# First convolution taps and two key scalings from VectorE to ScalarE, with both queues re-ordered, in a two-layer hybrid decoder step

## The chip, the cores and the metric

One core of one Trainium2 chip. The metric is the device time of one launch in microseconds (us); the median of the runs shown is what changes are judged by.

## The reference

A step of a decoder trunk of two layers over 320 tokens: a prompt of 256 and 8 sequences of 8 tokens with states. A layer is

```python
x = x + 0.5 * _swiglu(_rmsnorm(x, norm_ffn1), ...)
proj = _rmsnorm(x, norm_mix) @ w_in                  # split into four groups
o = concat[_rwkv7_group, _rglru_group, _gdn_group, _gla_group]
x = x + o @ w_out
x = x + 0.5 * _swiglu(_rmsnorm(x, norm_ffn2), ...)
```

The change touches two of the groups. In `_rwkv7_group`:

```python
kk = _l2norm(_heads(k * lp['rwkv_k_k'], HEAD_DIM))
k = k * (1.0 + (a - 1.0) * lp['rwkv_k_a'])
```

and in `_gdn_group` the causal convolution with `CONV_K = 4` taps over the 768 columns of q, k and v, ahead of a silu. All is float32.

## The kernel before

**Tiling.** Activations stand with their features on the 128 partitions and the 320 tokens along the free axis. Weights come in units of 128x1024 (eight blocks of 128x128), 166 units a layer: 66 for the first feed-forward part, 26 for the input projection (tiles 0 to 25 in this text), 8 for the output projection, 66 for the second feed-forward part. A float32 product is made of three matmuls on operands that are split in a high part (`wh`, `xh`) and a low part (`wl`, `xl`), lines L479 to L481; a tile of 128 output columns has 8 x 3 = 24 matmuls over 320 columns.

**How a unit gets there.** SyncE loads it to `raw` (a ring of four, from tile 14 on in two of these places) when the low part of the unit before in that place has been made. ScalarE copies it to `wh` (`split_hi`, L1186) when TensorE has used the unit that stood there four units earlier. VectorE subtracts to get `wl` (`split_lo`, L1592). TensorE waits for `lo_ready`, the count of low parts made. In the mixing stage `ahead(m)` makes the split of tile m + 4, on ScalarE and on VectorE alike: `ahead(5)` is the split of tile 9.

**The mixing stage** begins with the input projection. TensorE's order is written out by hand: tiles, with the small products of the four groups between them. Of its first part:

```python
tile_mm(layer, IN0 + 8, 0)
half_tile(layer, 9, 0)
rw_products(layer)
half_tile(layer, 9, 1)
...
rw_rows(layer)
...
tile_mm(layer, IN0 + 11, 1)
inverse_t(layer, 0, 1)
```

`half_tile(9, 0)` waits for the evacuation of tile 7 (`in_read` 8) and for the split of tile 9. Tiles 4 and up take turns in two banks, so tile m waits for the evacuation of tile m - 2. VectorE and ScalarE have orders written out by hand too, each a queue in which nothing is passed. VectorE's steps in the opening are: `evac(m)` (out of PSUM with the norm's factor, L1663 and L1664; it waits for tile m), `rw_mix` (token shift, L1683 to L1688), `rw_keys_raw` (L1693), `rw_keys` (L1696 to L1702), `rw_decay` (L1712, L1714), `rw_scaled` (L1718 to L1724), `gla_floor` (L1833, which waits for ScalarE's `gla_ab`, L1408), `rw_rest` (L1728, L1729; its products are read by `rw_products`), `rw_masks` (L1740, behind `rw_products`), `gdn_gate` (L1764 to L1770), `inverse(0, l)` (L1975, L1982 and a transpose L1967), `rw_reads` (L1707), `gdn_conv(j)` (the first tap L1752, the other three L1749), `gla_decay` (L1837, L1839). ScalarE's are: sigmoids (L1385, L1388), `kk_sq` (L1391), exponentials and logarithms of the decay and the key norm (L1393 to L1404, the last of them signals `kk_rn`), `gla_ab` behind `ahead(7)`, `eye(0)` (L1276, which waits on the count of splits up to tile 13, because it writes to places of the raw ring), the moves of `rw_rows` (L1292 and six times L1287), `inverse_t` (L1258) and `across` (L1266, L1267; `across(0, 1)` waits for `gla_decay`).

Of the kernel before, what the change touches and what calls it, by code (L numbers as in the profile page):

```python
# [16 lines left out]
ACT = mybir.ActivationFunctionType  # L17
ALU = mybir.AluOpType
# [5 lines left out]
NC = TOK // CH  # L24
# [4 lines left out]
CONV = 4  # L29
# [19 lines left out]
T_RW, T_SMALL, T_GDN, T_GLA, T_RG, T_Z, T_GT, T_RGG = 0, 3, 8, 14, 18, 20, 22, 24  # L49
# [30 lines left out]
def columns(spec):  # L80
# [28 lines left out]

MIX_SIGNALS = {  # L110
    "padded": ("pads", "rg_pads"), "xm": 7, "lora_in": 1, "lora_mm": 3, "sg": 2, "ra": 2,
    "rw_gc": 2, "shift_kept": 1, "kkraw": 2, "kk_sq": 1, "rkr": 2, "head_sums": ("kk_sum", "rk_sum", "gdn_sum"), "cum": 2, "prev": 1,
    "rw_P": 1, "kk_rn": 1, "rb": 1, "rw_ops": 1, "kPi": 1, "bPi": 1, "bonus": 1,
    "rw_pairs": 2, "rw_pairs_read": 6,
    "rw_rows_mm": 3, "rw_rows": 3, "conv": 6, "gdn_act": ("beta", "sp_dt", "cqk", "gsq", "cq", "gdn_ln", "gdn_rn"),
    "gates": 1, "gcum": 1, "gdn_spread": ("Gb_mm", "Gc_mm", "bb_mm"), "Gb": 2, "eG": 1,
# [8 lines left out]
    "hcen": 1, "yo": 1, "ysq0": 1, "ysq1": 1, "ysq2": 1, "cent_mm": 1, "cent_read": 1, "yrs": 3, "var_mm": 3, "VM": 4, "dec_mm": 3,  # L125
    "dec_decay": 3, "var_read": 3, "dec_add": 5, "sq_sum": 3,
}
V_STEPS, A_STEPS, G_STEPS = 102, 51, 14 + 3 * 6
G_ALL = DEPTH * G_STEPS - 6


# [44 lines left out]
def program(nc, xT, wts, par, cst, sin, mst, yT, sout, mout):  # L176
    with ExitStack() as ctx:
# [38 lines left out]
        def P(name, i=0, n=1):  # L216
            return pr[:, PAR[name][0] + i:PAR[name][0] + i + n]
# [90 lines left out]
        def chunked(v):  # L308
            return v.rearrange("q p (c t) -> q c p t", c=NC)
# [72 lines left out]
        S = {}  # L382
# [18 lines left out]
        def on(eng, layer, s, k=None):  # L401

            s = S[s] if isinstance(s, str) else s
            apart(eng, s, s.upto(layer, k)) if eng.engine in OWN_WAITS else eng.wait_ge(s.sem, s.upto(layer, k))
# [775 lines left out]
        def _(act):  # L1180
# [59 lines left out]
            for layer in range(DEPTH):  # L1240
                st = Steps(act, a_step, layer, plain)

                def say(ins, name):
                    return st(ins, S[name])
# [4 lines left out]
                def ahead(*ms):  # L1249
                    for m in ms:  # L1250
                        split_hi(layer, IN0 + RING + m)

                def inverse_t(g, l):
                    on(act, layer, f"inv_mm{g}", 2 * l - 1)
                    dst, src = pairs_of(Tm[g], l), products_of(l)
                    if l > 1:
                        dst, src = halves(dst, 1 << l, 0), halves(src, 1 << l, 0)
                    say(act.activation(dst, src, ACT.Copy), f"T{g}")  # L1258

                def across(g, l):  # L1260

                    on(act, layer, f"XY{g}", 2 * l - 1)
                    if (g, l) == (0, 1):
                        on(act, layer, "ltm_read")
                    n = chunks_of(l)
                    st(act.activation(Yx[g][half[1], 0:n], Y[g][half[0], NC:NC + n], ACT.Copy))  # L1266
                    say(act.activation(Yx[g][half[0], 0:n], Y[g][half[1], NC:NC + n], ACT.Copy), f"across{g}")  # L1267
# [5 lines left out]
                def eye(g):  # L1273
                    if g == 0:
                        act.wait_ge(lo_ready.sem, layer * UNITS + IN0 + LATE)
                    say(act.activation(Y[g], lev[:, 0, :].unsqueeze(1).broadcast_to([128, 10, CH]), ACT.Copy), f"eye{g}")  # L1276
# [5 lines left out]
                def home(dst, bank, name=None):  # L1282

                    for p in range(2):
                        for to, at in pieces(p):
                            d, n = dst[to, :, p, :], dst.shape[1]
                            ins = act.activation(d, ps[at, bank + p, 0:n * CH].rearrange("q (c t) -> q c t", c=n), ACT.Copy)  # L1287
                            say(ins, name) if name and to is half[1] else st(ins)
# [6 lines left out]
                def log_sums(dst, n):  # L1295
# [4 lines left out]
                            say(ins, "gdn_ln") if n == 4 and k == 1 and to is half[1] else st(ins)  # L1300
                    st.settle()

                def decode_out(g):
                    on(act, layer, "R0_mm", g + 1)
                    home(dec_out[g], 6, "R0T")
# [81 lines left out]
                for p in range(2):  # L1387
                    say(act.activation(ra[:, p, :], ps[:, 6 + p, 0:TOK], ACT.Sigmoid, bias=P("a0", p)), "ra")  # L1388
                ahead(4)
                act.wait_ge(S["kkraw"].sem, S["kkraw"].upto(layer))  # L1390
                say(act.activation(rsq[:], kk[:], ACT.Square), "kk_sq")  # L1391
                act.preload_act_table_set("natural_log_exp_and_others")
                st(act.activation(tiny[R, 10:11], P("alog")[R], ACT.Exp))  # L1393
                st(act.activation(lnt[R, :], small[R, :], ACT.Abs, bias=P("dtb")[R]))
                st(act.activation(tiny[:, 11:13], P("lam", 0, 2), ACT.Abs))
                ahead(5)
                act.wait_ge(S["cum"].sem, S["cum"].upto(layer))
                st(act.activation(rP[:], cum[:], ACT.Exp, scale=-WDEC))
                st(act.activation(Pinv[:], cum[:], ACT.Exp, scale=WDEC))
                act.wait_ge(S["prev"].sem, S["prev"].upto(layer))  # L1400
                say(act.activation(Pprev[:], sg[:], ACT.Exp, scale=-WDEC), "rw_P")
                act.wait_ge(S["kk_sum"].sem, S["kk_sum"].upto(layer))
                log_sums(rsq, 2)
                say(act.activation(rsq[:], rsq[:], ACT.Exp, scale=-0.5), "kk_rn")  # L1404
                ahead(6)
                ahead(7)
                on(act, layer, "gla_z")
# [10 lines left out]
                say(act.activation(tiny[:, 11:13], tiny[:, 11:13], ACT.Ln, bias=C("one")), "sp_lam")  # L1418
                say(act.activation(ltm, ltm, ACT.Ln, bias=C("one")), "gla_ln")
                ahead(8)  # L1420
                ahead(9)
                ahead(10)
                eye(0)
                on(act, layer, "rw_rows_mm", 1)
                rows_of(rVt, 2, "rw_rows")
                on(act, layer, "rw_rows_mm", 2)
                home(kLt, 4, "rw_rows")
                on(act, layer, "rw_rows_mm", 3)
                home(bLt, 6, "rw_rows")
                act.wait_ge(S["Gb_mm"].sem, S["Gb_mm"].upto(layer))  # L1430
                for p in range(2):
                    say(act.activation(Gb[:, p, :], ps[:, 6 + p, 0:TOK], ACT.Copy), "Gb")
                ahead(11)
                inverse_t(0, 1)
                across(0, 1)
                on(act, layer, "Gb")
                say(act.activation(eG[:], Gb[:], ACT.Exp), "eG")
                ahead(12)
                ahead(13)
                across(0, 2)  # L1440
                inverse_t(0, 2)
                act.wait_ge(S["conv"].sem, S["conv"].upto(layer, 4))
# [142 lines left out]
        def _(ve):  # L1585
# [62 lines left out]
            for layer in range(DEPTH):  # L1648
                st = Steps(ve, v_step, layer, plain)

                def say(ins, name):
                    return st(ins, S[name])
# [22 lines left out]
                def ahead(*ms):  # L1675
                    for m in ms:
                        split_lo(layer, IN0 + RING + m)
# [10 lines left out]
                        say(stt(seqs(xm[:, k, :], 0), seqs(xm[:, k, :], 0), P("mu", k), seqs(rwp[:, k, :], 1, 1), ALU.mult, ALU.add), "xm")  # L1688
                    st.settle()

                def rw_keys_raw():
                    for p in range(2):
                        say(ts(kk[:, p, :], xm[:, 2 + p, :], P("kk", p), -1.0, ALU.mult, ALU.mult), "kkraw")  # L1693

                def rw_keys():
                    st(ts(tiny[:, 13:15], P("ka", 0, 2), -1.0, 1.0, ALU.mult, ALU.add))  # L1696
                    on(ve, layer, "ra")
                    st.settle()
                    for p in range(2):
                        st(ts(kmod[:, p, :], ra[:, p, :], P("ka", p), tiny[:, 13 + p:14 + p], ALU.mult, ALU.add))  # L1700
                    st.settle()
                    st(tt(kmod[:], kmod[:], xm[:, 2:4, :], ALU.mult))  # L1702

                def rw_reads():
# [10 lines left out]

                def rw_scaled():
                    on(ve, layer, "kk_rn")
                    st(tt(kk[:], kk[:], rsq[:], ALU.mult))  # L1718
                    st.settle()
                    say(tt(ra[:], kk[:], ra[:], ALU.mult), "rb")  # L1720
                    on(ve, layer, "rw_P")
                    st(tt(kkr[:, :, :, 0, :], chunked(kk), chunked(Pprev), ALU.mult))
                    on(ve, layer, "rb")
                    say(stt(bPi[:], ra[:], -1.0, Pinv[:], ALU.mult, ALU.mult), "bPi")  # L1724

                def rw_rest():
                    on(ve, layer, "rw_P")
                    say(tt(kkr[:, :, :, 1, :], chunked(xm[:, 0:2, :]), chunked(rP), ALU.mult), "rw_ops")  # L1728
                    say(tt(kPi[:], kmod[:], Pinv[:], ALU.mult), "kPi")  # L1729
# [23 lines left out]

                def gdn_conv(j):
                    on(ve, layer, "shift_kept")
                    for k in range(CONV):
                        st.settle()
                        ins = tap(cv, gcp, j, 6, k, "gcw")
                        say(ins, "conv") if k == CONV - 1 else st(ins)

# [327 lines left out]
                evac(3)  # L2088
                rw_mix(2, 4)
                ahead(1)  # L2090
                rw_keys_raw()
                ahead(2)
                ahead(3)
                rw_decay()
                evac(4)
                rw_keys()
                evac(5)
                ahead(4)
                rw_mix(0, 2)
                ahead(5)  # L2100
                evac(6)
                rw_scaled()
                gla_floor()
                evac(7)
                rw_rest()
                ahead(6)
                evac(8)
                ahead(7)
                rw_mix(4, 6)
                ahead(8)  # L2110
                rw_masks()
                gdn_gate()
                ahead(9)
                evac(9)
                evac(10)
                ahead(10)
                inverse(0, 0)
                rw_reads()
                gdn_conv(0)
                gdn_conv(1)  # L2120
                gla_decay()
                evac(11)
                rw_gain()
                ahead(11)
# [411 lines left out]
```

## Time and profile before

| what | value |
|---|---|
| median of 3 runs | 1352.57 us (1351.97 to 1353.64) |
| profiled execution, its own time | 1353.87 us |
| its span | 1352.1 us, mean granted clock of TensorE 0.997 |
| busy: TensorE, VectorE, ScalarE, GpSimd | 1329.3, 855.8, 692.6, 77.4 us |
| weights read by SyncE's queue | 332 units of 512 KB |

The opening of the mixing stage, from the first evacuation to the end of the first group's inverse, lies at 255 to 330 us in layer 0 and at 922 to 997 in layer 1. Times of the trace count from the span's start. A timeline row has the start, the duration, engine, line and operation, and in brackets how long the engine had stood idle and what released it. Durations of neighbours overlap a little, so that what an instruction costs in a row of them is the distance between two starts. The end of a matmul is modelled.

### The profile page before, as it was taken

The numbers are of one execution on the slowest core, as the hardware profiler recorded it, in microseconds if no ns is written. First come the engines' busy times: TensorE is split into PE (matmuls) and PEld (weight loads), VectorE is DVE, ScalarE is ACT, GpSimd is POOL, SyncE is SP. The second block draws the span as 40 slices with busy tenths as digits, with TensorE's granted clock in tenths as the row PEclk, the third lists the DMA queues.
The fourth block names the chain that finished last, engine by engine and source line by source line (L and its number), as shares of the span: only waits on it lengthen the run. The fifth ranks groups of instructions, "written<-read, shape, count | busy, mean of one in ns | idle before, by whom it ended". The sixth has DMA issues, their size and how long they took to land.

```text
span 1352.1 us, 31424 instructions
## 1 busy us (share of the span) xinstructions
PE 1329.3 (98%) x12584; PEld 1289.2 (95%) x12584; DVE 855.8 (63%) x1327; ACT 692.6 (51%) x995; POOL 77.4 (6%) x113
## 2 busy tenths in 40 slices
PE   7999999999999999999999999999999999999997
PEld 7999999998988999999999999999888899999997
DVE  6656533898876756553376565349988766555533
ACT  7444423757655644443364444347466655454423
POOL 0000000200030100000010000001001310000001
PEclk9999999999999999999999999999999999999999
DMA  8544454322313644444454444443223244444541
GB/s 302 173 143 150 144 155 155 111 79 80 112 50 111 212 145 150 146 154 154 142 189 153 155 143 152 151 144 110 80 79 97 66 158 156 155 148 147 155 142 53
DMA packets 50768, 185.90 MB, mean 137 GB/s; under 512 B 5760, under 2 KB 6272, under 8 KB 50176
## 3 DMA queue, kind: packets, MB, share of 16 engines
q1 hardware_dynamic: 49104, 177.37, 41.3%
q10 hardware_dynamic: 1584, 7.35, 1.5%
q8 instruction: 63, 1.03, 0.3%
q14 instruction: 17, 0.14, 0.0%
HBM read 180.14 MB, written 4.56 MB: 137 GB/s over the span
## 4 chain that ended last, share of the span: by engine, by line
PE 86%; DVE 11%; issue 2%; ACT 1%; DMA 0%; DVEq 0%; ACTq 0%
PE ps L479 27%; PE ps L481 26%; PE ps L480 26%; DVE wl L1592 2%; DVE ar L1749 2%; PE ps L847 1%; DVE ar L1663 1%; PE ps L749 1%; PE ps L1035 0%; DVE raw L1967 0%; PE ps L817 0%; PE ps L1013 0%; PE ps L799 0%; DVE ar L1740 0%; DVE ar L1683 0%
## 5 line engine op out<-in xcount | busy, mean ns | idle before, releaser
L479 PE MATMUL ps<-xh,wh 128*128 128x320 f32 x1952 | 611.8, 313 | 9.0 <-DVE xl L1614 8.0
L1592 DVE TENSOR_TENSOR wl<-raw,wh 128x1024 fp32r<-128x1024 f32 x332 | 408.1, 1231 | 317.5 <-ACT wh L1186 317.1
L481 PE MATMUL ps<-xh,wl 128*128 128x320 f32 x1952 | 604.4, 310 | 0.0
L480 PE MATMUL ps<-xl,wh 128*128 128x320 f32 x1952 | 604.3, 310 | 0.0
L1186 ACT ACTIVATE wh<-raw 128x1024 fp32r<-128x1024 f32 x332 | 349.3, 1054 | 356.2 <-PE ps L481 339.1
L479 PEld LDWEIGHTS ps<-xh,wh 128*128 128x128 f32 x1952 | 367.5, 188 | 20.1 <-issue 9.0
L480 PEld LDWEIGHTS ps<-xl,wh 128*128 128x128 f32 x1952 | 367.7, 188 | 0.5
L481 PEld LDWEIGHTS ps<-xh,wl 128*128 128x128 f32 x1952 | 367.6, 188 | 0.0
L479 PE MATMUL ps<-hid_h,wh 128*128 (+1 forms) x704 | 217.5, 309 | 0.0
L480 PE MATMUL ps<-hid_l,wh 128*128 (+1 forms) x704 | 217.5, 309 | 0.0
L481 PE MATMUL ps<-hid_h,wl 128*128 (+1 forms) x704 | 217.5, 309 | 0.0
L1228 ACT ACTIVATE gus<-gus 128x320 f32<-128x320 f32 x88 | 41.6, 472 | 190.0 <-DVE gus L1631 190.0
L479 PEld LDWEIGHTS ps<-hid_h,wh 128*128 128x128 f32 x704 | 132.1, 188 | 0.0
L480 PEld LDWEIGHTS ps<-hid_l,wh 128*128 128x128 f32 x704 | 132.1, 188 | 0.0
L481 PEld LDWEIGHTS ps<-hid_h,wl 128*128 128x128 f32 x704 | 132.1, 188 | 0.0
L1631 DVE TENSOR_TENSOR gus<-ps,rstd 128x320 f32<-128x320 f32 x88 | 43.2, 491 | 97.0 <-PE ps L481 90.9
L2270 POOL TENSOR_TENSOR ar<-ar 128x320 f32<-128x320 f32 x35 | 30.7, 878 | 765.7 <-ACT ar L1211 758.0
L1228 ACT ACT_TABLE_LOAD x44 | 56.5, 1283 | 2.4 <-issue 1.6
L1635 DVE TENSOR_TENSOR gus<-gus 128x320 f32<-128x320 f32 x88 | 43.3, 492 | 16.0 <-ACT gus L1228 4.1
L1639 DVE TENSOR_TENSOR hid_l<-gus,hid_h 128x320 f32 x88 | 42.6, 484 | 0.0
L1632 DVE TENSOR_TENSOR gus<-ps,rstd 128x320 f32<-128x320 f32 x88 | 42.3, 481 | 0.0
L1614 DVE SCALAR_TENSOR_TENSOR xl<-x,pr,xh 128x320 fp32r<-128x320 f32 x48 | 39.5, 859 | 1.4 <-ACT xh L1210 1.4
(290 smaller groups left out, 934.6 us busy)
## 6 DMA issues: line engine op xcount, KB each, us to landing
raw<-wts SPq DMA_DIRECT2D x332, 512.0 KB, 3.5
ms<-mst ACTq DMA_DIRECT2D x2, 1440.0 KB, 7.9
mout<-ms ACTq DMA_DIRECT2D x2, 1440.0 KB, 6.6
x<-xT SPq DMA_DIRECT2D x4, 320.0 KB, 4.9
yT<-x SPq DMA_DIRECT2D x4, 320.0 KB, 2.4
cs<-cst SPq DMA_DIRECT2D x1, 652.0 KB, 8.1
pr<-par ACTq DMA_DIRECT2D x1, 429.0 KB, 4.2
pr<-par ACTq DMA_DIRECT2D x1, 425.0 KB, 5.3
```

The source lines that it names most:

```text
L479: pe.matmul(out, a, rh, start=start, stop=False)
L480: pe.matmul(out, a, rl, start=False, stop=False)
L481: return pe.matmul(out, b, rh, start=False, stop=stop)
L1186: act.activation(wh[:, s, :], raw_of(layer, n), ACT.Copy).then_inc(hi_ready.sem, 1)
L1228: act.activation(gus[:, m, :], gus[:, m, :], ACT.Silu).then_inc(sil_ready.sem, 1)
L1592: tt(wl[:, s, :], raw_of(layer, n), wh[:, s, :].bitcast(F32), ALU.subtract).then_inc(lo_ready.sem, 1)
L1614: stt(xl[:, k, :], x[:, k, :], P(name, k), xh[:, k, :].bitcast(F32), ALU.mult, ALU.subtract).then_inc(xl_ready.sem, 1)
L1631: tt(gus[:, m, :], ps[:, 2 * m, 0:TOK], rstd[:], ALU.mult).then_inc(gs_ready.sem, 1)
L1632: tt(gus[:, 2 + m, :], ps[:, 2 * m + 1, 0:TOK], rstd[:], ALU.mult).then_inc(gu_read.sem, 1)
L1635: tt(gus[:, m, :], gus[:, m, :], gus[:, 2 + m, :], ALU.mult).then_inc(act_ready.sem, 1)
L1639: tt(hid_l[:, at, :].rearrange("q a t -> q (a t)"), gus[:, m, :], hid_h[:, at, :].rearrange("q a t -> q (a t)").bitcast(F32), ALU.subtract ...
L2270: ins = gp.tensor_tensor(nsq[:, 0, :], nsq[:, 0, :], nsq[:, k, :], ALU.add)
```

## The change

- `kk_sq` is made on ScalarE from `xm` with the scale P("kk") in the square, in two instructions; VectorE's `rw_keys_raw` goes. `rw_scaled` multiplies the key in, in two instructions instead of one, and the sign moves from the key to `kkr` (two instructions instead of one) and out of `bPi`.
- The affine part of the modified key (`ka_mix`, two instructions of Identity with scale and bias) moves to ScalarE; VectorE keeps the small `rw_keys_rest` and one product.
- The first tap of each of the six convolution tiles (`first_tap(j)`, a Copy with a scale over 344 columns) moves to ScalarE. It waits for the evacuation of its tile and for a buffer. `gdn_conv(j)` waits for it and does taps 1 to 3.
- Both queues get another order. TensorE's, SyncE's and GpSimd's are as before.

```diff
@@ ScalarE
+                def first_tap(j):
+                    act.wait_ge(in_read.sem, in_read.upto(layer, T_GDN + j + 1))
+                    on(act, layer, "pads" if j < 3 else "bPi" if j < 5 else "rk_sum")
+                    say(act.activation(cv[:, j, 0:CVP - 3], gcp[:, j, 0:CVP - 3], ACT.Copy, scale=P("gcw", j)), "tap0")
...
-                act.wait_ge(S["kkraw"].sem, S["kkraw"].upto(layer))
-                say(act.activation(rsq[:], kk[:], ACT.Square), "kk_sq")
+                act.wait_ge(S["xm"].sem, S["xm"].upto(layer, 3))
+                for p in range(2):
+                    say(act.activation(rsq[:, p, :], xm[:, 2 + p, :], ACT.Square, scale=P("kk", p)), "kk_sq")
...
-                ahead(5)
                 act.wait_ge(S["cum"].sem, S["cum"].upto(layer))
                 st(act.activation(rP[:], cum[:], ACT.Exp, scale=-WDEC))
                 st(act.activation(Pinv[:], cum[:], ACT.Exp, scale=WDEC))
+                on(act, layer, "ra")
+                on(act, layer, "ka_rest")
+                for p in range(2):
+                    say(act.activation(kmod[:, p, :], ra[:, p, :], ACT.Identity, scale=P("ka", p), bias=tiny[:, 13 + p:14 + p]), "ka_mix")
...
                 say(act.activation(rsq[:], rsq[:], ACT.Exp, scale=-0.5), "kk_rn")
+                ahead(5)
                 ahead(6)
                 ahead(7)
...
                 ahead(8)
+                first_tap(0)
                 ahead(9)
+                eye(0)
                 ahead(10)
-                eye(0)
                 on(act, layer, "rw_rows_mm", 1)
                 rows_of(rVt, 2, "rw_rows")
...
                 home(bLt, 6, "rw_rows")
+                first_tap(1)
+                inverse_t(0, 1)
+                across(0, 1)
+                first_tap(2)
...
                 ahead(11)
-                inverse_t(0, 1)
-                across(0, 1)
...
                 ahead(12)
+                first_tap(3)
+                first_tap(4)
                 ahead(13)
+                first_tap(5)
@@ VectorE
-                def rw_keys_raw():
-                    for p in range(2):
-                        say(ts(kk[:, p, :], xm[:, 2 + p, :], P("kk", p), -1.0, ALU.mult, ALU.mult), "kkraw")
+                def rw_keys_rest():
+                    say(ts(tiny[:, 13:15], P("ka", 0, 2), -1.0, 1.0, ALU.mult, ALU.add), "ka_rest")
...
                 def rw_keys():
...
-                    for p in range(2):
-                        st(ts(kmod[:, p, :], ra[:, p, :], P("ka", p), tiny[:, 13 + p:14 + p], ALU.mult, ALU.add))
-                    st.settle()
+                    on(ve, layer, "ka_mix")
                     st(tt(kmod[:], kmod[:], xm[:, 2:4, :], ALU.mult))
...
                     on(ve, layer, "kk_rn")
-                    st(tt(kk[:], kk[:], rsq[:], ALU.mult))
+                    for p in range(2):
+                        st(stt(kk[:, p, :], xm[:, 2 + p, :], P("kk", p), rsq[:, p, :], ALU.mult, ALU.mult))
...
-                    st(tt(kkr[:, :, :, 0, :], chunked(kk), chunked(Pprev), ALU.mult))
+                    for p in range(2):
+                        st(stt(kkr[:, :, p, 0, :], kk[:, p, :].rearrange("q (c t) -> q c t", c=NC), -1.0,
+                               Pprev[:, p, :].rearrange("q (c t) -> q c t", c=NC), ALU.mult, ALU.mult))
...
                 rw_mix(2, 4)
                 ahead(1)
-                rw_keys_raw()
+                rw_keys_rest()
                 ahead(2)
                 ahead(3)
                 rw_decay()
                 evac(4)
-                rw_keys()
                 evac(5)
                 ahead(4)
                 rw_mix(0, 2)
-                ahead(5)
                 evac(6)
+                rw_keys()
                 rw_scaled()
                 gla_floor()
                 evac(7)
                 rw_rest()
+                ahead(5)
+                evac(8)
                 ahead(6)
-                evac(8)
+                rw_mix(4, 6)
                 ahead(7)
-                rw_mix(4, 6)
-                ahead(8)
                 rw_masks()
                 gdn_gate()
+                ahead(8)
+                evac(9)
                 ahead(9)
-                evac(9)
                 evac(10)
+                inverse(0, 0)
                 ahead(10)
-                inverse(0, 0)
+                gla_decay()
                 rw_reads()
                 gdn_conv(0)
                 gdn_conv(1)
-                gla_decay()
                 evac(11)
```

## Rows read from the trace of the kernel before

**Rows 1.** The page's first part: busy time, share of the span, instructions.

```profile
PE 1329.3 (98%) x12584; PEld 1289.2 (95%) x12584; DVE 855.8 (63%) x1327; ACT 692.6 (51%) x995; POOL 77.4 (6%) x113
```

**Rows 2.** TensorE's waits over the span: total us, times, longest us.

```profile
PE ps L904 <- issue: 1.2, 1, 1.2
PE ps L799 <- DVE raw L1967: 1.0, 2, 0.5
...
PE ps L479 <- DVE ar L1664: 1.0, 2, 0.5
...
PE ps L817 <- ACT ar L1267: 0.7, 2, 0.4
```

**Rows 3.** Busy time by stretch: PE, PEld, DVE, ACT, POOL, clock, DMA.

```profile
255.00:330.00 75.00, 73.61 (x880) 66.10 (x879) 71.63 (x140) 49.44 (x80) 3.66 (x9) 1.00 0.29 93
330.00:382.00 52.00, 52.00 (x1176) 46.75 (x1176) 43.17 (x87) 31.78 (x61) 7.71 (x13) 1.00 0.30 94
```

**Rows 4.** TensorE's timeline, 278 to 329 us.

```profile
278.71 0.31 PE L479 MATMUL ps<-xh,wh 128*128 128x320 f32 x1
...
293.02 0.41 PE L479 MATMUL ps<-xh,wh 128*128 128x320 f32 x1 [0.49 <-DVE ar L1664]
...
296.74 0.81 PE L799 MATMUL ps<-raw,ar 64*64 64x64 f32 x40
...
303.61 0.27 PE L817 MATMUL ps<-raw 64*64 64x64 f32 x2 [0.37 <-ACT ar L1267]
...
328.01 0.69 PE L799 MATMUL ps<-raw,ar 64*64 64x64 f32 x32 [0.53 <-DVE raw L1967]
```

**Rows 5.** Groups by line and form: busy us, mean ns of one.

```profile
L1210 ACT ACTIVATE xh<-x,pr 128x320 fp32r<-128x320 f32 x8 | 4.5, 558 | 1.0 <-DVE x L1595 1.0
...
L1752 DVE TENSOR_SCALAR ar<-ar,pr 128x344 f32<-128x344 f32 x6 | 2.4, 399 | 0.5
```

**Rows 6.** ScalarE's timeline, 275 to 277 us.

```profile
275.45 1.06 ACT L1186 ACTIVATE wh<-raw 128x1024 fp32r<-128x1024 f32 x1 [2.11 <-PE ps L481]
276.42 0.51 ACT L1408 ACTIVATE ar<-ps,pr 128x320 f32<-128x320 f32 x1
```

**Rows 7.** VectorE's timeline, 277 to 280 us.

```profile
277.35 0.54 DVE L1833 TENSOR_SCALAR ar<-ps,pr 128x320 f32<-128x320 f32 x1
277.81 0.41 DVE L1663 TENSOR_TENSOR ar<-ps,rstd 128x256 f32<-128x256 f32 x1
...
278.27 0.81 DVE L1728 TENSOR_TENSOR ar<-ar 128x640 f32<-128x640 f32 x1
...
279.74 1.31 DVE L1592 TENSOR_TENSOR wl<-raw,wh 128x1024 fp32r<-128x1024 f32 x1
```

**Rows 8.** VectorE's timeline, 282 to 292 us.

```profile
282.56 0.68 DVE L1683 TENSOR_TENSOR ar<-ar 128x512 f32<-128x512 f32 x1
...
284.79 1.22 DVE L1592 TENSOR_TENSOR wl<-raw,wh 128x1024 fp32r<-128x1024 f32 x1
285.93 3.13 DVE L1740 TENSOR_TENSOR ar<-ps,cs 128x512 f32<-128x512 f32 x6
289.10 0.38 DVE L1764 TENSOR_SCALAR ar<-ar,pr 4x320 f32<-4x320 f32 x1
...
291.28 1.22 DVE L1592 TENSOR_TENSOR wl<-raw,wh 128x1024 fp32r<-128x1024 f32 x1
```

**Rows 9.** ScalarE's timeline, 292 to 297 us.

```profile
292.54 0.74 ACT L1276 ACTIVATE raw<-cs 128x640 f32<-128x640 f32 x1 [0.76 <-DVE wl L1592]
293.18 0.69 ACT L1292 ACTIVATE ar<-ps 128x640 f32<-128x640 f32 x1
293.76 2.72 ACT L1287 ACTIVATE ar<-ps 128x320 f32<-128x320 f32 x6
```

**Rows 10.** Busy time by stretch in layer 1; the clock is the third number from the end.

```profile
995.00:1000.00 5.00, 4.97 (x48) 4.30 (x49) 3.04 (x4) 4.85 (x8) 0.00 (x0) 0.71 0.61 204
1000.00:1005.00 5.00, 5.00 (x61) 4.74 (x60) 2.51 (x6) 3.34 (x5) 0.00 (x0) 0.95 0.01 2
```

More of the change, by code:

```diff
@@ L111 @@
     "padded": ("pads", "rg_pads"), "xm": 7, "lora_in": 1, "lora_mm": 3, "sg": 2, "ra": 2,
-    "rw_gc": 2, "shift_kept": 1, "kkraw": 2, "kk_sq": 1, "rkr": 2, "head_sums": ("kk_sum", "rk_sum", "gdn_sum"), "cum": 2, "prev": 1,
-    "rw_P": 1, "kk_rn": 1, "rb": 1, "rw_ops": 1, "kPi": 1, "bPi": 1, "bonus": 1,
+    "rw_gc": 2, "shift_kept": 1, "kk_sq": 2, "rkr": 2, "head_sums": ("kk_sum", "rk_sum", "gdn_sum"), "cum": 2, "prev": 1,
+    "rw_P": 1, "kk_rn": 1, "rw_keyed": ("rb", "bPi", "rw_ops", "kPi"), "ka_mix": 2, "ka_rest": 1, "tap0": 6, "bonus": 1,
     "rw_pairs": 2, "rw_pairs_read": 6,
@@ L127 @@
 }
-V_STEPS, A_STEPS, G_STEPS = 102, 51, 14 + 3 * 6
+V_STEPS, A_STEPS, G_STEPS = 95, 51, 14 + 3 * 6
 G_ALL = DEPTH * G_STEPS - 6
@@ L1689, in rw_mix @@
                     st.settle()
-                def rw_keys_raw():
-                    for p in range(2):
-                        say(ts(kk[:, p, :], xm[:, 2 + p, :], P("kk", p), -1.0, ALU.mult, ALU.mult), "kkraw")
+                def rw_keys_rest():
+                    say(ts(tiny[:, 13:15], P("ka", 0, 2), -1.0, 1.0, ALU.mult, ALU.add), "ka_rest")
                 def rw_keys():
-                    st(ts(tiny[:, 13:15], P("ka", 0, 2), -1.0, 1.0, ALU.mult, ALU.add))
-                    on(ve, layer, "ra")
-                    st.settle()
-                    for p in range(2):
-                        st(ts(kmod[:, p, :], ra[:, p, :], P("ka", p), tiny[:, 13 + p:14 + p], ALU.mult, ALU.add))
-                    st.settle()
+                    on(ve, layer, "ka_mix")
                     st(tt(kmod[:], kmod[:], xm[:, 2:4, :], ALU.mult))
@@ L1721, in rw_scaled @@
                     on(ve, layer, "rw_P")
-                    st(tt(kkr[:, :, :, 0, :], chunked(kk), chunked(Pprev), ALU.mult))
+                    for p in range(2):
+                        st(stt(kkr[:, :, p, 0, :], kk[:, p, :].rearrange("q (c t) -> q c t", c=NC), -1.0,
+                               Pprev[:, p, :].rearrange("q (c t) -> q c t", c=NC), ALU.mult, ALU.mult))
                     on(ve, layer, "rb")
-                    say(stt(bPi[:], ra[:], -1.0, Pinv[:], ALU.mult, ALU.mult), "bPi")
+                    say(tt(bPi[:], ra[:], Pinv[:], ALU.mult), "bPi")
                 def rw_rest():
@@ L1755, in gdn_conv @@
                     on(ve, layer, "shift_kept")
-                    for k in range(CONV):
-                        st.settle()
+                    on(ve, layer, "tap0", j + 1)
+                    for k in range(1, CONV):
+                        if k > 1:
+                            st.settle()
                         ins = tap(cv, gcp, j, 6, k, "gcw")
```

## The prediction

> **What bounds the kernel now.** I read the page first. TensorE is busy 98% of the span [rows 1], so a change can give back only what TensorE loses, and can cost only what it makes TensorE lose. The second view is the list of TensorE's waits [rows 2]: three of them lie in the opening of the mixing stage, where this change is, each once per layer. The third is the busy time by stretch [rows 3]: in the 75 us of the opening (255 to 330) TensorE lacks 75.00 - 73.61 = 1.39 us and VectorE is busy 71.63 of 75, ScalarE 49.44. In the next 52 us VectorE has nearly 9 us free. So in the opening TensorE and VectorE run side by side with almost no play. The timeline shows where TensorE is held, in brackets behind a row [rows 4]: 0.49 us ahead of tile 11 (for `evac(9)`), 0.37 us ahead of `inverse_y(0, 1)` (for `across(0, 1)`, which waits for `gla_decay`), 0.53 us ahead of `inverse_t(0, 4)`. Sum 1.39 us a layer, 2.8 us in all: that is the most that the opening can give, 0.2% of the time, as long as the clock is the same.
>
> **What the change takes off VectorE.** A start-to-start distance is what an instruction costs in a row of them. Two key scalings (an estimate of 0.7 us at nearly the price of a first tap; a small instruction takes their place), two affine instructions (0.8), six first taps at 0.40 us and a short settling each (2.6) [rows 5]: 3.9 us less with the small one taken off. `rw_scaled` gets two instructions for one at two places, some 0.2 us more each. Net VectorE is 3.4 us shorter a layer. That alone would more than pay the 1.39 us.
>
> **What it puts on ScalarE.** An instruction over 320 columns with its scale read from a tile took 0.558 us [rows 5]; so six taps 3.4 us, `ka_mix` 1.1, and `kk_sq` 0.3 more. The trace has no Identity with scale and bias both from a tile: bounds 0.46 and 0.65, I take 0.56. ScalarE has 25 us free in the opening, so the 4.8 us are hidden, unless one stands ahead of something due. `kk_rn` does not come later: `ahead(5)`, 0.95 us, now stands behind it and pays for `ka_mix`.
>
> By the Trainium skill, "ScalarE: Activation LUTs", Rules for kernel authors, a multiplication belongs on VectorE and not on ScalarE. The rows agree as to the price, 0.40 us against 0.56. By that rule alone the six taps lose 1 us a layer; by the sum here they cost nothing where ScalarE is idle.
>
> **The new order: a wait at tile 9.** TensorE starts half tile 9 only when its split is done, and `ahead(5)` is that split. Before, VectorE made it ahead of `evac(6)` and TensorE ran through from tile 8, with the first matmul of tile 9 at 278.71 [rows 4]. Now `ahead(5)` stands behind `rw_keys`, `rw_scaled`, `gla_floor`, `evac(7)` and `rw_rest`, while TensorE's order is the same. When does VectorE come to it?
> - `evac(6)` waits for tile 6. Tile 7 ended at 275.4 (it released ScalarE's split [rows 6]) and a tile takes 3.5 us (tile 11 has 296.74 - 293.02 = 3.72 with 0.1 of switching at either end [rows 4]), so tile 6 ends at 271.9. From there `evac(6)` 0.46, `rw_keys` 0.74, the two key instructions 1.0, `rb` 0.74, two for `kkr` 1.0, `bPi` 0.74: 276.6. 0.46 is the distance of one evacuation and 0.74 that of a 640-column instruction, half of `rw_rest`'s 1.47 [rows 7]; the 1.0 are estimates at 0.5 for an instruction of 320 columns, between 0.40 and 0.58. The strided pair for `kkr` isn't in the trace; between 0.48 and 0.8 each, I take 0.5; the low end changes nothing here and the high end adds 0.3 us of wait.
> - `gla_floor` needs `gla_ab` of ScalarE, which ends at 276.42 + 0.51 = 276.93 and hangs on tile 7 by way of `ahead(7)` [rows 6], unchanged. So VectorE, arriving at 276.6, waits until 276.94.
> - `gla_floor` and `evac(7)` 0.92, `rw_rest` 1.47, the split 1.2 to 1.3 [rows 7]: 276.94 + 0.92 + 1.47 + 1.23 = 280.56.
>
> TensorE goes on at 280.6 and not at 278.71: **1.9 us lost**, and 0.1 for the restart (the first matmul behind a wait takes 0.41 instead of 0.31 us [rows 4]). It is 2.0 us behind. Even if `gla_ab` were early, VectorE's own work would leave 1.6 us.
>
> **A second wait, at `inverse_t(0, 1)`.** It needs ScalarE's `rw_rows`, which now stand behind `eye(0)` and `ahead(10)`, and `eye(0)` waits for VectorE's `ahead(9)`. VectorE from 279.33 (the start of `ahead(5)`): split 1.14 (285.93 - 284.79), `evac(8)` 0.46, split 1.14, `rw_mix(4, 6)` 2.23, split 1.14, masks 3.17 and about 0.3 of wait for the second group of pair products (TensorE being late), `gdn_gate` 2.18, split 1.14, `evac(9)` 0.46, split 1.22 to its end [rows 7, 8]: 14.6 us, so 293.9. Then ScalarE: `eye(0)` 0.64 to the next start, the split 0.95, the rows 3.30 (293.18 to 293.76 + 2.72) [rows 9]: 298.8. They were done at 296.48. TensorE itself would be there at 296.74 + 2.0 - 0.49 = 298.25, because tile 11 no longer waits. So it waits 0.6 us and is then 2.1 us behind.
>
> **What comes back.** `gla_decay` is now ahead of the taps, so `across(0, 1)` is done at 301.5, while TensorE needs it at 305: the 0.37 us go. VectorE is back on the old times at 322 (its relief has been spent in waits for TensorE), and TensorE comes to `inverse_t(0, 4)` late: the 0.53 us go too. The load of raw tile 17 hangs on `ahead(11)`, which ends some 0.6 us later than before; its tile is due well after. First taps 3 to 5 wait for evacuations that come before ScalarE's next split is allowed by TensorE, so they hold up nothing. Behind 330 VectorE and ScalarE are the ones that wait, and the later waits in [rows 2] are chains through TensorE itself; nothing there takes up the rest. Balance per layer 2.0 - 0.49 + 0.6 - 0.37 - 0.53 = **1.2 us, 2.4 us in two layers**.
>
> **The clock.** After the wait at `inverse_t(0, 4)` of layer 1 and four thin matmuls, the granted clock fell to its lower level: 0.71 in one stretch of 5 us and 0.95 in the next [rows 10]. By the clock that is 5.00 x (0.29 + 0.05) = 1.7 us of full-clock work. The same place in layer 0 had no fall, so it is a matter of chance. The profiled execution took 1353.87 us, 1.30 over the median of 1352.57, so I take the median run as one without a fall. A wait of 1.9 us is over three times that of 0.53, and 0.6 us now stand just ahead of the thin matmuls of `gdn_decay`. I count one more fall in the median run at 1.6 us, with none to three as bounds.
>
> The Trainium skill, "TensorE: Matmul & The Clock Gate", The HAM clock gate, says that the array's clock is throttled by default and that activity releases it, with two levels only. The trace agrees with two levels; that rule would make the fall likelier with longer idling, as assumed above.
>
> **The forecast and the rivals.** A difference below 0.2%, 2.7 us, can't be told from none.
> - **A, 0.48: the wait at tile 9, and the clock falls more often.** 1352.57 + 2.4 + 1.6 = 1356.6, own range 1355.3 to 1359.6 (up to three falls).
> - **B, 0.27: the wait at tile 9, no more falls.** 1355.0. For it: a 1.2 us wait late in the recurrences [rows 2] had no fall behind it. Within 0.2%.
> - **C, 0.12: the relief reaches TensorE.** It decides at the start of `ahead(5)`: if VectorE gets there at 277.5 and not 279.3, nothing is lost at tile 9, and with it the second wait goes. The gain is then 1.39 us a layer, and layer 1's fall with its wait: 1352.6 - 2.8 = 1349.8 or less, faster. For it: VectorE's waits for TensorE could be shorter than I put them. Against it: `gla_ab` alone forbids 277.5.
> - **D, 0.13: ScalarE's queue becomes the path.** Its taps stand ahead of splits and of `rw_rows`; a tap that waits for an evacuation holds all behind it. Were `eye(0)`, `ahead(10)` and the rows another 1 us later, this adds 1 us a layer to A or B: 1357 to 1359. Slower. The table of rules named above points that way.
>
> **Slower** is A and D, 0.61; **the same** is B, 0.27; **faster** is C, 0.12. The range 1352.0 to 1359.6 leaves out most of C and the far end of D, and takes in a bound of one layer's balance near zero.
>
> **What would show it.** In the profile after, in both layers: a wait of TensorE for the split L1592 of about 1.9 us between the 72 matmuls of tiles 6 to 8 and the half tile, a wait for `rw_rows` ahead of L799 of about 0.6 us, and none of the three old ones. VectorE idle ahead of `evac(6)` for about 1 us and ahead of `gla_floor`. The prediction is wrong if half tile 9 starts without a wait, if VectorE runs ahead of these times, or if something behind 330 takes up the delay.

## The result and the profile after

The changed kernel took 1361.8 us (1357.09 to 1365.68, 7 runs) against 1352.77 (1351.97 to 1354.28, 7 runs) of the kernel before beside it: ratio 1.0063, 95% interval 1.0042 to 1.0083. It is slower by 9.0 us. The forecast was slower, but with 1356.6 us and no more than 1359.6: the sign holds and the size does not.

The profiled execution is the fastest of the seven, 1357.09 us, span 1355.2 us, mean clock 0.998.

The page's first part, which answers to [rows 1]:

```profile
PE 1329.4 (98%) x12584; PEld 1289.3 (95%) x12584; DVE 849.1 (63%) x1311; ACT 701.7 (52%) x1013; POOL 77.2 (6%) x113
```

TensorE is busy for the same time. What was added in this execution is idle time: 1355.2 - 1329.4 = 25.8 us against 22.8. VectorE has 6.7 us less to do, ScalarE 9.1 more. TensorE's waits, as in [rows 2]:

```profile
PE ps L479 <- DVE wl L1608: 3.9, 2, 1.9
PE ps L799 <- ACT ar L1287: 2.8, 2, 2.1
...
PE ps L904 <- issue: 0.6, 1, 0.6
```

The three waits of the old opening are gone, two new ones stand in their place, and both are the ones of the prediction. TensorE's timeline at them, layer 0 and then layer 1:

```profile
280.96 0.38 PE L479 MATMUL ps<-xh,wh 128*128 128x320 f32 x1 [1.93 <-DVE wl L1608]
...
299.24 0.81 PE L799 MATMUL ps<-raw,ar 64*64 64x64 f32 x40 [0.68 <-ACT ar L1287]
...
947.94 0.39 PE L479 MATMUL ps<-xh,wh 128*128 128x320 f32 x1 [1.94 <-DVE wl L1608]
...
967.66 0.81 PE L799 MATMUL ps<-raw,ar 64*64 64x64 f32 x40 [2.12 <-ACT ar L1287]
```

1.93 and 1.94 us were forecast as 1.9, and 0.68 as 0.6. But in layer 1 the second wait is 2.12 us. The chain of the work that ended last, followed through layer 1 up to that wait (start, duration, what), names what is new:

```profile
958.34 1.24 DVE wl L1608
959.58 0.02 issue
959.59 3.65 DMA raw<-wts
963.24 0.02 issue
963.26 1.06 ACT wh L1186
964.32 0.59 ACT ar L1292
```

`ahead(8)` on VectorE, the split of tile 12, ends at 959.58. Only then does SyncE load tile 14, which lands 3.65 us later; ScalarE has done `eye(0)` and stands before `ahead(10)`, which is tile 14's split, and behind it are the rows of `rw_rows` for which TensorE waits. ScalarE's timeline shows the stop, layer 0 without it and layer 1 with it:

```profile
294.21 0.74 ACT L1276 ACTIVATE raw<-cs 128x640 f32<-128x640 f32 x1 [3.63 <-DVE wl L1608]
294.85 1.04 ACT L1186 ACTIVATE wh<-raw 128x1024 fp32r<-128x1024 f32 x1
295.80 0.69 ACT L1292 ACTIVATE ar<-ps 128x640 f32<-128x640 f32 x1
296.39 2.71 ACT L1287 ACTIVATE ar<-ps 128x320 f32<-128x320 f32 x6
...
961.20 0.74 ACT L1276 ACTIVATE raw<-cs 128x640 f32<-128x640 f32 x1 [3.64 <-DVE wl L1608]
963.26 1.06 ACT L1186 ACTIVATE wh<-raw 128x1024 fp32r<-128x1024 f32 x1 [1.33 <-DMA raw<-wts]
```

Why only layer 1: up to tile 13 a unit goes to the raw place of its number modulo four, and tile 14 goes to place 0 in both layers. 66 units stand ahead of tile 0 in layer 0, 232 in layer 1, so the unit that last held place 0 is tile 10 in layer 0 and tile 12 in layer 1. Tile 12's split is one of those that the change moved, behind `gdn_gate`.

Busy time by stretch, for [rows 3] and beyond, first the kernel after, with its stretches in layer 1:

```profile
255.00:330.00 75.00, 72.39 (x877) 65.46 (x875) 68.32 (x133) 54.31 (x89) 3.76 (x9) 1.00 0.28 93
375.00:425.00 50.00, 47.90 (x1095) 41.34 (x1092) 35.85 (x81) 30.64 (x53) 13.21 (x17) 1.00 0.16 54
...
922.00:997.00 75.00, 70.95 (x829) 63.98 (x829) 66.48 (x131) 51.57 (x85) 3.73 (x9) 0.98 0.27 86
...
965.00:970.00 5.00, 2.88 (x53) 1.86 (x54) 4.79 (x9) 4.40 (x10) 0.00 (x0) 1.00 0.28 109
970.00:975.00 5.00, 5.00 (x29) 4.39 (x22) 3.65 (x7) 3.02 (x6) 0.00 (x0) 0.66 0.14 15
```

and then two more stretches of the kernel before (375 to 425 holds the recurrences of layer 0):

```profile
375.00:425.00 50.00, 47.07 (x1051) 40.72 (x1052) 35.96 (x80) 29.91 (x50) 13.21 (x17) 1.00 0.14 45
...
922.00:997.00 75.00, 73.61 (x881) 66.10 (x879) 71.67 (x140) 49.44 (x80) 3.68 (x9) 1.00 0.30 93
```

Layer 0's opening loses 73.61 - 72.39 = 1.22 us more than before, where the prediction had 1.2. Layer 1's opening loses 73.61 - 70.95 = 2.66 us more. Behind its long wait the clock fell: 0.66 over 5 us, which is 5.00 x 0.34 = 1.7 us of full-clock work. The kernel before had its one fall between 995 and 1005 [rows 10], so the openings of the two profiled executions have a fall each, and nearly all of the 1357.09 - 1353.87 = 3.2 us between them is idle time.

In the recurrences of layer 0 TensorE idles 2.10 us instead of 2.93, 0.8 us less. That is no effect of the delay as far as the traces show. `late12_alone` (below), whose opening of layer 0 is that of before, idles 1.71 us there (the first row), and a second execution of the changed kernel, `after_again`, 2.40 (the second):

```profile
375.00:425.00 50.00, 48.29 (x1096) 41.89 (x1091) 36.45 (x81) 31.29 (x52) 13.21 (x17) 1.00 0.14 45
375.00:425.00 50.00, 47.60 (x1089) 40.45 (x1086) 35.40 (x81) 29.96 (x52) 13.23 (x17) 1.00 0.16 53
```

The other runs of the changed kernel differ in the clock. A thousandth of the mean granted clock over 1,360 us is 1.4 us of full-clock work:

```
us      1357.09  1357.62  1361.03  1361.80  1363.30  1363.75  1365.68
clock   0.998    0.998    0.995    0.995    0.993    0.993    0.993
```

The median run has 0.003 less than the profiled one, 4.1 us by the clock (to within 1.4 us, as both are rounded to a thousandth), and is 4.7 us longer. So 9.0 us are: 3.2 of idle time in the profile, 4.7 from there to the median run of after, and 1.1 from the profiled run of before (which has a fall) down to its median.

### The profile page after: what moved, and what is told of

Read it like the earlier page. It is cut to its first block, busy times and chain, and to the rows that moved or that the text cites. A ratio compares the mean times of both kernels' runs of the same rounds, so it can differ in the third digit from the quotient of the medians.

```text
span 1355.2 us, 31438 instructions
## 1 busy us (share of the span) xinstructions
PE 1329.4 (98%) x12584; PEld 1289.3 (95%) x12584; DVE 849.1 (63%) x1311; ACT 701.7 (52%) x1013; POOL 77.2 (6%) x113
## 4 chain that ended last, share of the span: by engine, by line
PE 95%; DVE 2%; ACT 1%; issue 1%; DMA 1%; DVEq 0%; ACTq 0%
PE ps L479 29%; PE ps L480 28%; PE ps L481 28%; PE ps L657 1%; PE ps L847 1%; PE ps L817 1%; PE ps L799 1%; PE ps L749 1%; DVE wl L1608 1%; DMA raw<-wts 1%; PE ps L1035 0%; PE ps L1013 0%; ACT wh L1186 0%; PE ps L633 0%; PE ps L775 0%
```

## The experiments

Each kernel was run beside the kernel before on the same chip; times are medians.

**Which part of the change loses the time?** The moved operations were run alone, in the order of before (`ka_mix` right behind the sigmoids that it reads), on two chips; and the order alone, with the operations of before.

```diff
 # ops_only, ops_only_again: after, with before's order of both queues
 act:  ahead(8)  first_tap(0)  ahead(9)  ahead(10)  eye(0)
       rows_of(...)  home(bLt, 6, "rw_rows")  first_tap(1)
       ahead(11)  inverse_t(0, 1)  across(0, 1)  first_tap(2)
 # order_only: before, with after's order of both queues
 ve:   evac(6)  rw_keys()  rw_scaled()  gla_floor()  evac(7)  rw_rest()  ahead(5)
 act:  ahead(9)  eye(0)  ahead(10)  ...  inverse_t(0, 1)  across(0, 1)  ahead(11)
```

> The moved operations of the change in the order of the kernel before (ka_mix right behind ra). Theory W (the loss is all in the new order: two waits of TensorE, and the clock falls that they bring): no wait at tile 9 or at inverse_t(0, 1), the three old waits of 1.39 us a layer mostly gone, so 1350.0 to 1351.5, faster than before by 1 to 2.5 us. Rival O (the moved operations themselves cost, ScalarE's queue being the path): slower than before by 1 us or more, with TensorE waiting for ScalarE in the opening.

> The moved operations in the order of before, a second time. If the first result holds: 1349.5 to 1350.7, no wait of TensorE over 0.25 us in the opening of either layer, and no low clock there. If it was this chip's or that hour's: 1352 to 1353.

> The kernel before with its own operations, in the changed kernel's order on VectorE and ScalarE (no first taps, key scalings on VectorE). Theory O (the order makes the whole loss, and the moved operations give back nearly 3 us in either order): waits of 2.0 to 2.5 us at half tile 9 and 1 to 4.5 us at inverse_t(0, 1), median 1361 to 1366, at or above the changed kernel's. Rival Q (the moved operations cost something once they stand in ScalarE's queue in the new order): the second wait is under 1 us in both layers and the median is 1354 to 1359, below the changed kernel's.

Measured: the operations alone 1350.2 us (1348.66 to 1351.69) against 1352.96, ratio 0.9978 (0.9969 to 0.9987), and 1350.07 against 1353.42 on another chip, 0.9976 (0.9966 to 0.9985): faster than both kernels. The order alone 1362.27 (1360.03 to 1362.79), ratio 1.0063 (1.0049 to 1.0077), the changed kernel's ratio. Busy time by stretch of the operations alone, both openings:

```profile
255.00:330.00 75.00, 74.71 (x888) 67.28 (x887) 69.87 (x136) 57.01 (x94) 4.21 (x10) 1.00 0.33 102
922.00:997.00 75.00, 74.71 (x888) 67.27 (x887) 68.73 (x131) 57.02 (x94) 3.58 (x6) 1.00 0.31 98
```

TensorE idles 0.29 us instead of 1.39 in each: 2.2 of the 2.8 us that the prediction named as the most there is. The medians gained 2.8 and 3.4 us; what stands beside the 2.2 was not traced, but neither opening of `ops_only` has a fall of the clock. The order alone waits, by TensorE's list:

```profile
PE ps L479 <- DVE wl L1592: 4.6, 2, 2.3
PE ps L799 <- ACT ar L1287: 2.6, 2, 1.9
```

Its second wait is 0.7 us in layer 0 and 1.9 in layer 1, where 1 to 4.5 was expected. So the order makes the whole loss. The moved operations make the wait at tile 9 0.4 us shorter (2.3 to 1.9), but in the new order that does not show in the medians: 1362.27 and 1361.8, in separate groups of runs. The rival by which they cost something in ScalarE's queue falls.

**Which step of the order?** One split of VectorE was moved, alone, in the kernel before (`late9_alone`, `late12_alone`), or put back in the changed kernel (`split9_back`, `split12_back`, `both_back`).

```diff
 # late9_alone, in before: ahead(5) behind rw_rest
-                ahead(5)
                 evac(6)
 ...
                 rw_rest()
+                ahead(5)
 # late12_alone, in before: ahead(8) behind gdn_gate
-                ahead(8)
                 rw_masks()
                 gdn_gate()
+                ahead(8)
 # split9_back, in after: ahead(5) between rw_keys and rw_scaled
 # split12_back, in after: ahead(8) ahead of rw_masks
 # both_back: both
```

> The kernel before with one thing of the change: VectorE's split of tile 9 (ahead(5)) behind rw_rest. VectorE then works 1.1 us later at that place than in the changed kernel's walk would have it only from gla_floor on, so the wait at half tile 9 is 1.7 to 2.3 us in both layers. Theory: the other waits of before shrink, since VectorE ends its masks at the same time as before, and TensorE is late; net 0.3 to 0.8 us a layer, with a fall or two of the clock: 1354 to 1356. Rival (each idle wait of 2 us brings a fall of the clock at once): 1356.5 or more, and two falls in the profile.

> The kernel before with another one thing of the change: VectorE's split of tile 12 (ahead(8)) behind gdn_gate. Theory L: layer 0 keeps its opening (the load of tile 14 hangs on tile 10 there); in layer 1 the load of tile 14 starts some 5.5 us later, ScalarE stands at ahead(10) until about 3.7 us behind that split, and TensorE waits 2.5 to 3.5 us at inverse_t(0, 1), with the clock low for one to three times 3.4 us: 1356 to 1361. Rival (a load is hidden by the ring anyway): within 1 us of before.

> The changed kernel with VectorE's split of tile 12 (ahead(8)) back ahead of the masks. Theory L (in layer 1 the raw place of tile 14 is that of tile 12, so that its load starts only behind this split, and ScalarE stands at ahead(10) for the landing): the second wait of layer 1 falls from 2.1 to about 0.7 us and layer 0 stays, so the profile is 1.3 us shorter at the same clock and the median 1 to 3 us under 1361.8. Rival: the second wait of layer 1 is VectorE's lateness and stays at about 2 us.

> The changed kernel with VectorE's split of tile 9 (ahead(5)) ahead of rw_scaled. Theory W2 (the second wait hangs on VectorE's chain from gla_floor on and not on the first wait): no wait at tile 9, but the wait at inverse_t(0, 1) grows from 0.7 to 1.5 to 2.3 us in layer 0, and TensorE is 0.3 to 1 us earlier there than in the changed kernel; one long wait a layer fewer, so median 1355 to 1359. Rival: the second wait was a follow-up of the first and goes with it: 1350 to 1353.

> The changed kernel with VectorE's splits of tiles 9 and 12 both back (ahead(5) ahead of rw_scaled, ahead(8) ahead of the masks). Theory: no wait at half tile 9 beyond 0.5 us and none for the load, but the wait for rw_rows behind eye(0) and ahead(10) stays in both layers, 1.5 to 2 us, as TensorE is there earlier: 1353 to 1356. Rival (the two splits were the whole loss): 1350 to 1351.5, as with the moved operations in the old order.

In the table "none" is none over 0.25 us.

| kernel | us | ratio (95%) | wait at tile 9, layers 0 and 1 | at `inverse_t(0, 1)` |
|---|---|---|---|---|
| `late9_alone` | 1355.78 | 1.0027 (1.0017 to 1.0036) | 1.93, 1.94 | none |
| `late12_alone` | 1360.19 | 1.0056 (1.0043 to 1.0069) | none | none, 4.4 |
| `split12_back` | 1354.89 | 1.0014 (1.0005 to 1.0023) | 1.93, 1.94 | none, 0.4 |
| `split9_back` | 1361.91 | 1.0070 (1.0057 to 1.0083) | 0.44, 0.44 (for `evac(7)`) | 1.9, 4.4 |
| `both_back` | 1357.01 | 1.0030 (1.0018 to 1.0041) | 0.45, 0.44 (for `evac(7)`) | 1.91, 1.91 |

One split moved in the kernel before costs nearly as much as the whole change: `late12_alone`, in which layer 0's opening is as it was. ScalarE's timeline there, and the busy time by stretch around the wait:

```profile
962.54 1.06 ACT L1186 ACTIVATE wh<-raw 128x1024 fp32r<-128x1024 f32 x1 [7.97 <-DMA raw<-wts]
963.50 0.72 ACT L1276 ACTIVATE raw<-cs 128x640 f32<-128x640 f32 x1
```

```profile
965.00:970.00 5.00, 2.43 (x42) 2.02 (x43) 4.62 (x8) 2.30 (x6) 0.00 (x0) 0.71 0.32 107
970.00:975.00 5.00, 5.00 (x20) 3.09 (x19) 4.81 (x10) 3.55 (x7) 0.00 (x0) 0.50 0.02 5
975.00:980.00 5.00, 5.00 (x63) 4.74 (x62) 2.22 (x5) 1.49 (x2) 0.00 (x0) 0.76 0.30 105
```

ScalarE stands 7.97 us for the load, TensorE 4.4 us for the rows (2.5 to 3.5 were expected; the load took 4.79 us, against 3.65 in the changed kernel), and the clock is low for some 10 of these 15 us: 5.00 x (0.29 + 0.50 + 0.24) = 5.2 us of full-clock work, which is more than the wait. All five runs had a mean clock of 0.994 or 0.995.

`split12_back` was expected 1 to 3 us under the changed kernel, with layer 0 as it was, and came 6.9 us under (in separate groups of runs; ratio 1.0014 against 1.0063): the direction held, the size did not. In layer 1 the load's part of the wait is gone. In layer 0 the second wait is gone too, but in this profile a fall behind tile 9 had made TensorE later: the rows were done at 300.6 and TensorE came at 301.1.

`split9_back` was expected at 1355 to 1359 and missed. It takes away 1.5 us of the wait at tile 9 in each layer, and the second wait takes most of it back. TensorE comes there 1.4 us earlier, measured from `evac(6)`, and VectorE's split of tile 12 only 0.2 us: in layer 0 the wait is 1.91 us instead of 0.68. In layer 1 the load, which here took 4.68 us, came on top: 4.4 instead of 2.1. Behind it the clock was low again, by the stretches 5.00 x (0.10 + 0.50 + 0.42) = 5.1 us:

```profile
965.00:970.00 5.00, 0.62 (x18) 0.43 (x19) 3.58 (x6) 4.66 (x9) 0.00 (x0) 0.90 0.35 123
970.00:975.00 5.00, 5.00 (x49) 2.64 (x44) 3.92 (x9) 3.88 (x8) 0.00 (x0) 0.50 0.10 40
975.00:980.00 5.00, 5.00 (x23) 5.00 (x23) 1.67 (x2) 0.75 (x2) 0.00 (x0) 0.58 0.36 105
```

`both_back` was expected at 1353 to 1356 and missed by 1 us: without the load the rows are still late, behind `eye(0)` and `ahead(10)`, by 1.91 us in both layers. Which of the moves that are left makes this wait was not tried. Its profile, the longest of its eight runs, has falls of 1.7 us of work in layer 0 and 3.4 in layer 1.

**Is it the load, or the queues?** The orders of the changed kernel were kept, and in layer 1 the raw places of tiles 10 and 12 were exchanged, so that tile 14's load hangs on tile 10's split as in layer 0.

```diff
+        if u == UNITS + IN0 + 10:
+            s = 0
+        elif u == UNITS + IN0 + 12:
+            s = 2
         mine = held.setdefault(s, [])
 ...
-                stream(done, late)
+                stream(done, late - 4)
+                for u in range(late - 4, late):
+                    one(u)
```

> The changed kernel with every engine's order as it is; in layer 1 alone, tiles 10 and 12 of the input projection change their raw places, so that the load of tile 14 hangs on the split of tile 10, as in layer 0, and no longer on that of tile 12. Theory L (the long second wait of layer 1 is this load): that wait goes from 2.1 us to 0.7, as in layer 0, the stretches at the lower clock behind it become rare, and the median is 1355 to 1358. Rival S (ScalarE's and VectorE's queues alone make the second wait, the load is a bystander): the wait stays at 2 us or more, and the median at 1360 to 1363.

Measured: 1357.67 us (1356.38 to 1358.54), ratio 1.0032 (1.0020 to 1.0044); mean clock 0.996 to 0.998. TensorE's waits, and ScalarE in layer 1 (lines are 6 higher here):

```profile
PE ps L485 <- DVE wl L1614: 3.9, 2, 1.9
PE ps L805 <- ACT ar L1293: 1.4, 2, 0.7
```

```profile
965.76 0.74 ACT L1282 ACTIVATE raw<-cs 128x640 f32<-128x640 f32 x1 [3.63 <-DVE wl L1614]
966.40 1.05 ACT L1192 ACTIVATE wh<-raw 128x1024 fp32r<-128x1024 f32 x1
```

The second wait is 0.7 us in both layers and ScalarE no longer stops for a DMA. No instruction of a compute engine was moved. The ratio falls from 1.0063 to 1.0032, 4 us, of which 2.12 - 0.68 = 1.4 are the wait. The rest is put down to the clock: its profile has no fall behind the second wait (though one behind each of those at tile 9), and no run's mean clock is under 0.996. `split12_back` gives back 2.4 us more, of which 1.0 is waits by the profiles (0.69 + 0.68 - 0.38).

**Is the rest the clock?** The changed kernel was run again on another chip; and in `filled` TensorE was given matmuls to do during the two waits (12 ahead of half tile 9, 4 in layer 0 and 13 in layer 1 ahead of `inverse_t(0, 1)`). They write a bank of PSUM that is free there, and nothing reads them.

```diff
+                    on(pe, layer, in_read, 8)
+                    filler(1, 12)
                     half_tile(layer, 9, 0)
 ...
+                    on(pe, layer, in_read, 11)
+                    filler(0, 4 if layer == 0 else 13)
                     inverse_t(layer, 0, 1)
```

> The changed kernel once more, for a second trace and more times. Theory K (what lies between its fastest run, 1357.09, and its median, 1361.8, is time at the lower clock that follows the two waits): the runs' mean granted clock goes down as their time goes up, 0.998 at 1357 and 0.993 at 1363 to 1366; a profile at 1361 or more has 3 to 5 falls of 3.4 us in the opening, most of them in layer 1 behind inverse_t(0, 1), and its waits are as long as in the first profile. Rival M (the waits themselves, on landings of loads, are longer in slow runs): the clock stays at 0.998 and the wait at inverse_t(0, 1) of layer 1 is 4 us or more.

> The changed kernel with matmuls that nobody reads put into the two new waits of TensorE: 12 of 0.147 us ahead of half tile 9, and 4 (layer 0) or 13 (layer 1) ahead of inverse_t(0, 1). The waits stay, but TensorE is not idle in them. Theory F (the timed runs are far over the profiled execution because the clock falls after the idle waits): median 1355 to 1357.5 and a narrow spread, 4 to 6 us under the changed kernel's 1361.8, no stretch below full clock in the opening. Rival N (the excess has another cause, such as loads or waits that vary between runs): median stays at 1360 or more.

`after_again` took 1361.36 us, the median of six, and the ratio is 1.0064 (1.0050 to 1.0078), over five of them: 1357.77, 1358.99, 1360.17, 1362.55 and 1362.99 at clocks of 0.997, 0.997, 0.996, 0.994 and 0.994. The sixth took 4,570 us, and why was not found. Time and clock go together again, but no long run of this kernel was profiled. One of `order_only` was: it has the changed kernel's order and ratio, and its profiled execution is its median, 1362.27 us. Its span is 1360.5 - 1352.1 = 8.4 us over that of before, of which 4.4 are idle time and 1333.3 - 1329.3 = 4.0 are a TensorE that is busy for longer. The low clock lies behind the wait at tile 9 in both layers and behind the second wait of layer 1:

```profile
280.00:285.00 5.00, 2.81 (x11) 2.84 (x12) 4.96 (x10) 1.98 (x4) 2.14 (x4) 0.73 0.29 93
285.00:290.00 5.00, 5.00 (x83) 4.63 (x81) 3.60 (x7) 0.00 (x0) 0.00 (x0) 0.92 0.71 223
950.00:955.00 5.00, 3.64 (x16) 3.34 (x18) 4.93 (x11) 1.16 (x2) 1.30 (x3) 0.66 0.31 105
975.00:980.00 5.00, 5.00 (x27) 4.90 (x24) 4.47 (x9) 2.27 (x4) 0.00 (x0) 0.66 0.02 5
```

That is 5.00 x (0.27 + 0.08 + 0.34 + 0.34) = 5.2 us of full-clock work in three falls, against 1.7 in one before.

`filled` took 1359.05 us (1357.12 to 1361.96), ratio 1.0049 (1.0037 to 1.0061), where 1355 to 1357.5 was expected: missed, though it is not at the rival's 1360 either. TensorE's time by stretch shows the waits filled and no low clock:

```profile
255.00:330.00 75.00, 74.71 (x869) 67.78 (x871) 68.61 (x133) 54.21 (x89) 3.91 (x10) 1.00 0.29 93
922.00:997.00 75.00, 74.79 (x866) 68.05 (x865) 68.14 (x133) 53.22 (x87) 3.91 (x10) 1.00 0.29 87
```

Four of its six runs had a clock of 0.999, at 1357.12 to 1359.4 us; the median is 2.7 us under the changed kernel's, taken in separate groups of runs, and the intervals of the two ratios overlap. The delay itself stays, since fillers give nothing back. The profile supports the clock's part: no fall is left. The time shows it weakly: 2.3 us lie between runs of one and the same clock, and for those I have no cause. In the profiled one TensorE idled 3.38 us between 1040 and 1095, in the recurrences of layer 1, and in the changed kernel's 1.86.

## Why the prediction was right and wrong

**Right: the wait at tile 9.** 1.93 and 1.94 us for 1.9. Its steps hold too. VectorE's timeline in layer 0, which is the walk of the prediction:

```profile
272.10 0.43 DVE L1679 TENSOR_TENSOR ar<-ps,rstd 128x256 f32<-128x256 f32 x1 [1.42 <-PE ps L481]
...
273.30 1.01 DVE L1729 SCALAR_TENSOR_TENSOR ar<-ar,pr 128x320 f32<-128x320 f32 x2
...
275.09 0.89 DVE L1734 SCALAR_TENSOR_TENSOR ar<-ar 128x320 f32<-128x320 f32 x2
...
277.12 0.55 DVE L1848 TENSOR_SCALAR ar<-ps,pr 128x320 f32<-128x320 f32 x1 [0.41 <-ACT ar L1418]
...
279.52 1.30 DVE L1608 TENSOR_TENSOR wl<-raw,wh 128x1024 fp32r<-128x1024 f32 x1
```

VectorE comes to `gla_floor` at 276.7 (276.6 forecast), waits for ScalarE, and starts the split at 279.5 (279.33); TensorE is on these times some 0.3 us later than in the trace before. `late9_alone` shows this wait without the rest of the change: 1355.78 us, +0.27%, with one fall of the clock behind it in its profile.

**Right: the second wait in layer 0**, 0.68 us for 0.6, with `eye(0)` at 294.2 (293.9) and the rows done at 299.1 (298.8), and the three old waits gone. **Right: costs on ScalarE** of the taps, 0.576 us each for 0.56, hidden. `ops_only` shows that the relief of VectorE was real and would have reached TensorE in the old order. Case C failed by the order alone; case D, a queue of ScalarE that becomes the path, came true in layer 1, though by a load and not by a tap.

**Wrong, the step that failed first: the balance of 1.2 us a layer, doubled to "2.4 us in two layers".** It was worked out on the times of layer 0, and the only load in it is that of raw tile 17. The load that matters is tile 14's: in layer 1 it hangs on `ahead(8)`, which the new order put behind `gdn_gate`. The second wait of layer 1 was 2.12 us for the 0.6 of the sum, and the openings together lost 1.22 + 2.66 = 3.9 us for 2.4. `places_swapped`, which takes only this away, gives 1357.67 us, 4.3 us over its own before where the forecast had 4.0.

**Wrong: the clock, "one more fall in the median run at 1.6 us".** The size of a fall was right, the number was not. Clock and spread measured 4.7 + 1.1 = 5.8 us by the sum over the runs (of which 4.1 + 1.1 stand by the mean clock and the one fall), which is the work of three falls and not of one. `order_only`, at the same ratio, shows three in its openings. The assumption that a longer wait makes a fall likelier held. In the profiles with the wait of 1.9 to 2.3 us at tile 9 there was a fall behind 7 of 12 such waits, and behind the waits of 1.8 to 2.1 us at `inverse_t(0, 1)` behind 4 of 6. The changed kernel has three waits of this length in a run, and the prediction gave the median run one fall and took three as the bound.

**Not shown wrong: "nothing there takes up the rest".** Behind 330 the profile after idles 0.8 us less in the recurrences of layer 0, and L904's wait went from 1.2 us [rows 2] to 0.6. But the kernel with layer 0's old opening has 1.2 us less there too, so this is no mark of the delay.

By size: idle time 3.2 us for 2.4 (3.9 in the openings, 0.8 less in the recurrences), clock and spread 5.8 for 1.6; 9.0 for 4.0.

**Open:** the spread of 2.3 us at one clock in `filled`; why the recurrences idle more in one execution than in the next; why one load took 3.3 us and another 4.8; and whether what TensorE does behind a wait, small products or large ones, changes how long the clock stays low. No run varied that by itself.

## What to carry to other kernels

When a split, a copy or any other step that frees a buffer is moved, follow what is loaded into that buffer, in each layer or iteration on its own: where units rotate over four places and a layer has a number of them that four does not divide, the same line frees another tile. On a kernel that TensorE bounds, move operations between engines first and leave the order; judge a new order by when each step is due and not by its owner's load. And price a wait of TensorE with the low clock behind it, for each wait by itself: in `order_only` it cost 4.0 us beside 4.4 of idle time, and behind the waits of 4.4 us more than the wait.

## What the runs showed of the hardware

- Full-clock work was lost in pieces of some 1.7 us, in some executions and not in others. Behind waits of 0.4 to 0.7 us in the openings there was one such piece in all profiles [rows 10]. Behind the wait of 1.9 to 2.3 us at tile 9 it was there in 7 of 12 places: none of 2 in the changed kernel, 1 of 2 in `after_again`, `late9_alone` and `split12_back`, 2 of 2 in `order_only` and `places_swapped`. Behind waits of 1.8 to 2.1 us at `inverse_t(0, 1)` it was there in 4 of 6, once doubled (`both_back`, layer 1: 0.82 and 0.50 over two stretches of 5 us). Behind 4.4 us it was 5.1 and 5.2 us in two kernels.
- One load of 512 KB took 3.65 us from the end of the split that frees its place to its landing; the same load took 3.32 in `after_again`, 3.40 in `order_only`, 4.68 in `split9_back` and 4.79 in `late12_alone`.
- TensorE's idle time in the recurrences of layer 0 differs between executions of one kernel: 2.10 and 2.40 us in the changed kernel, 2.39 and 1.95 in the moved operations alone (375 to 425).
- ScalarE's Identity with scale and bias both from a tile took 1.19 us for two over 320 columns, with 1.09 to the next start: 0.55 each, as one with a scale alone.
